# Six of eight gate/up K-tiles of an expert in three passes, low parts written over the raw weights, three slots per weight piece

## What is computed

```python
def rms_norm(x, g):
    y = xf * lax.rsqrt(jnp.mean(xf * xf, axis=-1, keepdims=True) + EPS)
    return y * g
def hier_moe(h, w_rg, b_rg, w_re, b_re, w_g, w_u, w_d):
    ...
    hid = jax.nn.silu(jnp.einsum('bsd,edf->bsef', h, w_g)) * jnp.einsum('bsd,edf->bsef', h, w_u)
    hid = hid * gate[..., None]
    return jnp.einsum('bsef,efd->bsd', hid, w_d)
for l in range(DEPTH):
    x = x + hybrid_mixer(rms_norm(x, norm_mix_g[l]), ...)
    x = x + hier_moe(rms_norm(x, norm_ffn_g[l]), ...)
```

## Time and profile before

| | |
|---|---|
| median of 3 runs | 1399.3 us (1398.26 to 1400.98) |
| profiled execution, its own time | 1398.75 us |
| its span | 1396.8 us |
| TensorE matmul busy | 1363.1 us (98%), granted clock 0.993 |
| VectorE / ScalarE / GpSimd busy | 863.2 (62%) / 585.8 (42%) / 728.4 us (52%) |
| DMA | 224.28 MB, mean 161 GB/s |

### The profile page before, as it was taken

How to read it: one execution, slowest core, us unless ns; L and a number is a source line. 1 busy time by engine, 2 the same in 40 slices (tenths; PEclk the granted TensorE clock), 3 DMA queues, 4 the chain that set the end, 5 groups by cost and what they waited for, 6 DMA issues and landing times.

```text
span 1396.8 us, 19901 instructions
## 1 busy us (share of the span) xinstructions
PE 1363.1 (98%) x6916; PEld 1036.2 (74%) x6916; DVE 863.2 (62%) x2057; ACT 585.8 (42%) x1334; POOL 728.4 (52%) x587
## 2 busy tenths in 40 slices
PE   7999999999999999999889999999999999999997
PEld 5788877777777876767477888777777778667674
DVE  4487866656684347776346787666567741576772
ACT  4323333343433135676443432433434421466761
POOL 4566645445345634566555576454444455255663
PEclk9999999999999999999889999999999999999999
DMA  5436422222212659999732242222222128599995
GB/s 154 130 100 172 121 83 73 73 74 97 90 61 76 232 217 318 340 360 350 190 118 76 61 135 81 75 76 74 89 80 90 61 88 292 213 330 350 346 348 130
DMA packets 148570, 224.28 MB, mean 161 GB/s; under 512 B 18635, under 2 KB 95877, under 8 KB 148463
## 3 DMA queue, kind: packets, MB, share of 16 engines
q1 hardware_dynamic: 136030, 197.59, 43.6%
q0 software_dynamic: 9936, 16.81, 5.1%
q10 hardware_dynamic: 2496, 8.52, 1.6%
HBM read 215.47 MB, written 31.25 MB: 177 GB/s over the span
## 4 chain that ended last, share of the span: by engine, by line
PE 92%; DVE 4%; ACT 1%; POOL 1%; DMA 1%; issue 1%; SPq 0%; POOLq 0%; ACTq 0%; DVEq 0%
PE bank L895 22%; PE bank L897 21%; PE bank L896 21%; PE bank L1200 9%; PE bank L1071 4%; PE bank L1083 3%; PE bank L1104 2%; PE bank L1152 2%; PE bank L1024 1%; PE bank L1094 1%; DVE probs L1913 1%; PE bank L1037 1%; POOL w_lo L769 1%; PE bank L1162 1%; PE bank L1360 0%
## 5 line engine op out<-in xcount | busy, mean ns | idle before, releaser
L769 POOL TENSOR_TENSOR w_lo<-raw,w_hi 128x512 fp32r<-128x512 f32 (+2 forms) x288 | 359.2, 1268 | 16.4 <-ACT w_hi L1641 4.6
L763 POOL TENSOR_SCALAR w_hi<-raw 128x1024 fp32r<-128x1024 f32 (+2 forms) x142 | 149.4, 1052 | 417.3 <-PE bank L897 414.5
L896 PE MATMUL bank<-w_hi,hT_lo 128*128 128x512 f32 (+2 forms) x696 | 258.8, 372 | 0.0
L895 PE MATMUL bank<-w_lo,hT_hi 128*128 128x512 f32 (+2 forms) x576 | 216.8, 376 | 2.1 <-DVE hT_lo L1738 1.2
L897 PE MATMUL bank<-w_hi,hT_hi 128*128 128x512 f32 (+2 forms) x576 | 211.8, 368 | 0.0
L895 PE MATMUL bank<-hT_lo,w_hi 128*128 128x512 f32 x384 | 159.5, 415 | 0.0
L897 PE MATMUL bank<-hT_hi,w_hi 128*128 128x512 f32 x384 | 150.7, 393 | 0.0
L896 PE MATMUL bank<-hT_hi,w_lo 128*128 128x512 f32 x384 | 150.2, 391 | 0.0
L896 PEld LDWEIGHTS bank<-w_hi,hT_lo 128*128 128x128 f32 x696 | 131.6, 189 | 20.3
L1200 PE MATMUL bank<-work,ptmp 128*128 128x512 f32 x288 | 129.4, 593 | 1.0 <-ACT ptmp L1565 1.0
L895 PEld LDWEIGHTS bank<-w_lo,hT_hi 128*128 128x128 f32 x576 | 108.7, 189 | 28.0 <-issue 8.7
(11 more groups left out here) (331 smaller groups left out, 2651.4 us busy)
## 6 DMA issues: line engine op xcount, KB each, us to landing
work<-in_w_ff_gate SPq DMA_DIRECT2D x66, 512.0 KB
work<-in_w_ff_up SPq DMA_DIRECT2D x66, 512.0 KB
work<-in_w_ff_down SPq DMA_DIRECT2D x33, 1024.0 KB
raw<-in_w_gate SPq DMA_DIRECT2D x48, 512.0 KB, 3.8
raw<-in_w_in SPq DMA_DIRECT2D x40, 512.0 KB, 3.6
raw<-in_w_branch SPq DMA_DIRECT2D x24, 512.0 KB, 3.6
raw<-in_w_out SPq DMA_DIRECT2D x16, 512.0 KB, 3.9
normed_dram<-mixed ACTq DMA_DIRECT2D x8, 512.0 KB, 2.7
```

Of the source, the lines that this page charges most:

```text
L763: nc.gpsimd.tensor_scalar(w_hi[:, two, :, 0:w], raw[:, slot, :, 0:w], 1.0, 0.0, ALU.mult, ALU.add).then_inc(split_hi, 1)
L769: last = nc.gpsimd.tensor_tensor(w_lo[:, two, kk, 0:w], raw[:, slot, kk, 0:w], w_hi[:, two, kk, 0:w].bitcast(F32), ALU.subtract)
L895: nc.tensor.matmul(out_ap, s_hi, m_lo, start=start, stop=False)
L896: nc.tensor.matmul(out_ap, s_lo, m_hi, start=False, stop=False)
```

## The change

Six of eight gate/up K-tiles of an expert go in three passes where four did (tiles 2 to 7, before 4 to 7), from expert 1 on instead of expert 2 (`SPLIT_FROM = 2`, `FIRST_SPLIT = 1`); tiles are split in pairs. Low parts are written over the raw weights they come from (`slots_low` are the same bytes as `slots_raw`), so a slot comes free only when TensorE has used it. There are nine slots, three per piece: the ring's six, two in `X` and one in `w_lo`. For the two in `X` the loads wait until `X` is stored, turned and scaled. Gate/up weights are loaded with two consecutive rows of 256 floats per partition, one run of 2 KB instead of 1 KB. The norm's gain, before a scale on ScalarE and VectorE in each expert, is now multiplied into `xn` once by GpSimd (8 products of 128x512, reading every second element so that the columns stand in the order of the weights' rows; one of them after the power step). The high parts of expert 1's tiles are made by ScalarE before `et_out(0)`, and their low parts by GpSimd before its loop over the experts. The one-hot tiles and token picks move to other places of `hT_lo`.

```diff
-RING = 6
+SLOTS_OF_PART = ((0, 3, 6), (1, 4, 7), (2, 5, 8))
+AHEAD = 3
+
+ROW_RUN = 2
 
 EXPERT_AT = [PER_GROUP * (e % N_GROUPS) + e // N_GROUPS for e in range(N_EXPERTS)]
 PIECES = 3
 
-FIRST_SPLIT = 2
-
-PIECE_ORDER = [(2, 0), (2, 1), (2, 2), (3, 0), (3, 1), (4, 1)]
-for before in range(2, N_EXPERTS - 1):
-    PIECE_ORDER += [(e, part) for e, part in ((before + 2, 0), (before + 1, 2), (before + 3, 1)) if e < N_EXPERTS]
-
-
-def split_count(e):
-
-    return 4 * (e - FIRST_SPLIT + 1)
+FIRST_SPLIT, SPLIT_FROM = 1, 2
+SPLIT_PAIRS = (8 - SPLIT_FROM) // 2
+
+PIECE_ORDER = [(2, 2), (2, 0), (2, 1), (3, 0), (3, 1)]
+for e in range(4, N_EXPERTS):
+    PIECE_ORDER += [(e, 0), (e, 1), (e - 1, 2)]
+PIECE_ORDER.append((N_EXPERTS - 1, 2))
...
+        X_low = low_twin("X_low", [P, TT, D_MODEL], F32R)
         X = sb("X", [P, TT, D_MODEL])
...
+        w_lo_raw = low_twin("w_lo_raw", [P, 2, UNIT_KT, 512], F32)
...
-        both = hT_hi[:, 4, 0:64].rearrange("p (t e) -> p t e", t=TT)
-        pick_token = hT_hi[:, 4, 64:192].rearrange("p (k t e) -> p k t e", k=2, t=TT)
+        both = hT_lo[:, 5, 0:64].rearrange("p (t e) -> p t e", t=TT)
+        pick_token = hT_lo[:, 5, 64:192].rearrange("p (k t e) -> p k t e", k=2, t=TT)
...
+        ffn_gain = probs[:, 0:2, :].rearrange("p a n -> p (a n)")
...
-        slot_onehot = hT_hi[:, 5:7, :].rearrange("p a (t s) -> p a t s", s=CAPACITY)
+        slot_onehot = hT_lo[:, 6:8, :].rearrange("p a (t s) -> p a t s", s=CAPACITY)
...
-        et_hi, et_lo = hT_hi[:, 0:2, :], hT_hi[:, 2:4, :]
-        gu_hi_bufs = [[oT_hi[:, k, :] for k in range(4)], [hT_lo[:, k, :] for k in range(4)]]
-        gu_lo_bufs = [[oT_lo[:, k, :] for k in range(4)], [hT_hi[:, 5, :], hT_hi[:, 6, :], hT_hi[:, 7, :], hT_lo[:, 6, :]]]
+        et_hi = hT_hi[:, 0:4, :].rearrange("p (b a) n -> p b (a n)", b=2)
+        et_lo = ptmp_low[:, :, :].rearrange("p (b a) n -> p b (a n)", b=2)
+        gu_hi_bufs = [[oT_hi[:, 0:2], oT_hi[:, 2:4], oT_lo[:, 0:2], oT_lo[:, 2:4]],
+                      [hT_lo[:, 0:2], hT_lo[:, 2:4], hT_hi[:, 4:6], hT_hi[:, 6:8]]]
+        slots_raw = [work[:, n].rearrange("p k n -> p (k n)") for n in range(6)]
+        slots_raw += [X[:, 0:2, :].rearrange("p a n -> p (a n)"), X[:, 2:4, :].rearrange("p a n -> p (a n)"),
+                      w_lo_raw[:, :, :, :].rearrange("p a k n -> p (a k n)")]
...
+            return src.rearrange("a (j p k) n -> p (a j) (k n)", p=P, k=ROW_RUN)
...
-                    slot, old = n % RING, e - 2
+                    old = e - AHEAD
                     if old >= 0 and part == 0:
                         sp.wait_ge(first_half, old + 1)
-                    elif old >= 0 and part == 1 and splits(old):
-                        sp.wait_ge(gu_lo, split_count(old))
                     elif old >= 0 and part == 1:
                         sp.wait_ge(gu_done, old + 1)
                     elif old >= 0:
-                        sp.wait_ge(down_lo, old + 2)
-                        if old:
-                            sp.wait_ge(down_lo_dve, old)
+                        sp.wait_ge(down_done, 2 * (old + 1))
                     if part < 2:
                         for half, w in enumerate((w_ff_gate, w_ff_up)):
                             src = layer_of(w, l)[:, EXPERT_AT[e], part * 512:(part + 1) * 512, :]
-                            sp.dma_start(gate_up_piece(slot)[:, half],
-                                         src.rearrange("a (k p) n -> p (a k) n", p=P)).then_inc(piece_in[slot], 16)
+                            sp.dma_start(gate_up_piece(e, part)[:, half].rearrange("p (j k) n -> p j (k n)", k=ROW_RUN),
+                                         in_runs(src)).then_inc(arrived(e, part), 16)
                     else:
-                        sp.dma_start(work[:, slot].rearrange("p (k c) n -> p k (c n)", k=2),
+                        sp.dma_start(down_rows(e),
...
                 sp.wait_ge(g_free, 4 * OUT_CHUNK)
+                sp.dma_start(ffn_gain, layer_of(norm_ffn_g, l).broadcast_to([P, D_MODEL])).then_inc(gain_in, 16)
...
+                    if (e, part) == (2, 0):
+                        sp.wait_ge(x_stored, 16 * TT)
+                        sp.wait_ge(x_gained, 2 * TT)
+                        sp.wait_ge(nt_done, 2 * KT)
                     load_piece(e, part)
...
-                        if i < 2:
+                        at = N_EXPERTS + i
+                        if i < AHEAD:
                             used, per = ((first_half, 1), (gu_done, 1), (down_done, 2))[part]
-                            sp.wait_ge(used, per * (N_EXPERTS - 1 + i))
+                            sp.wait_ge(used, per * (at - AHEAD + 1))
                         else:
                             used, per = ((e_gu, 1), (e_gu, 1), (e_down, 2))[part]
-                            sp.wait_ge(used, per * (i - 1))
...
+                def gain_step(t, c):
+                    pool.wait_ge(g_free, 4 * (OUT_CHUNK + c) + t + 1)
+                    cols = slice(c * 512, (c + 1) * 512)
+                    in_order = lambda rows: rows.rearrange("p (a n k) -> p a k n", n=P, k=ROW_RUN)
+                    nc.gpsimd.tensor_tensor(xn[:, t, cols].rearrange("p (a k n) -> p a k n", n=P, k=ROW_RUN),
+                                            in_order(X[:, t, cols]), in_order(ffn_gain[:, cols]),
+                                            ALU.mult).then_inc(x_gained, 1)
+
+                pool.wait_ge(gain_in, 32)
+                for t in range(TT):
+                    gain_step(t, 0)
+                for t in range(TT - 1):
+                    gain_step(t, 1)
                 pool.wait_ge(ms_done, TT + 1)
                 pow_step(row_rs[:, 1, :], row_ms[:, 1, :], TT).then_inc(rs_done, 1)
+                gain_step(TT - 1, 1)
...
-                            last = nc.gpsimd.tensor_tensor(w_lo[:, c, f, :], rows[:, f, c * 512:(c + 1) * 512],
+                            last = nc.gpsimd.tensor_tensor(down_low(e)[:, f, c * 512:(c + 1) * 512],
+                                                           rows[:, f, c * 512:(c + 1) * 512],
                                                            w_hi[:, c, f, :].bitcast(F32), ALU.subtract)
...
+                for n, (part, kk, kt) in enumerate(split_tiles()):
+                    pool.wait_ge(gu_hi, n + 1)
+                    for k in range(2):
+                        last = nc.gpsimd.tensor_tensor(
+                            gate_up_low(1, part)[:, :, kk + k, :], gate_up_piece(1, part)[:, :, kk + k, :],
+                            pair_hi_of(1, kt)[:, k, :].bitcast(F32).rearrange("p (h n) -> p h n", h=2), ALU.subtract)
+                    last.then_inc(gu_lo, 1)
...
+                if e and first_native(e):
+                    pe.wait_ge(et_act, copied(e))
...
+                for kt in range(KT):
+                    part, kk = divmod(kt, 4)
+                    if kk == 0:
+                        pe.wait_ge(arrived(e, part), loaded(e, part))
+                    rows = slice(kt * P, (kt + 1) * P)
+                    if kt < first_native(e):
+                        if e == 0 and kt < 4:
+                            pe.wait_ge(et_first, kt + 1)
                         if e == 0 and kt == 2:
                             turn_rest_of_first()
                         if e == 0 and kt == 4:
                             pe.wait_ge(et_dve, 1)
+                        last = nc.tensor.matmul(G[e % 2][:, :], et[:, e % 2, rows], gate_up_piece(e, part)[:, :, kk, :],
+                                                start=(kt == 0), stop=(kt == KT - 1))
+                    else:
+                        pair = (kt - SPLIT_FROM) // 2
+                        if kt == SPLIT_FROM:
+                            pe.wait_ge(et_dve, e + 1)
+                        if (kt - SPLIT_FROM) % 2 == 0:
+                            pe.wait_ge(gu_lo, split_pairs(e - 1) + pair + 1)
+                        last = three(G[e % 2][:, :], et_hi[:, e % 2, rows], et_lo[:, e % 2, rows],
+                                     pair_hi_of(e, kt)[:, (kt - SPLIT_FROM) % 2, :], gate_up_low(e, part)[:, :, kk, :],
+                                     kt == 0, kt == KT - 1)
+                    if kk == 3:
+                        last.then_inc(gu_done if part else first_half, 1)
...
+                native = P * min(4, first_native(e))
+                if native:
+                    nc.scalar.activation(et[:, e % 2, 0:native], S[0][:, 0:native], ACT.Copy).then_inc(et_act, 1)
                 if splits(e):
+                    if native < 512:
+                        nc.scalar.activation(et_hi[:, e % 2, native:512], S[0][:, native:512],
+                                             ACT.Copy).then_inc(et_hi_done, 1)
                     act.wait_ge(et_turned, 2 * e + 2)
-                    nc.scalar.activation(et_hi[:, e % 2, :], S[1][:, :], ACT.Copy).then_inc(et_hi_done, 1)
```

(75 more changed lines are left out.)

118 lines of the change are left out of this document (59 added, 59 removed).

## The result

The changed kernel takes **1414.15 us** (median of 4 runs, 1413.64 to 1414.25), the kernel before beside it 1399.62 (1398.26 to 1400.98). The ratio is 1.0104, 95% interval 1.0091 to 1.0117: 1% slower. The forecast was 1389, range 1386 to 1396. The profiled execution has a span of 1412.4 us, 15.6 more than before.

What follows compares the result with a forecast made beforehand. TensorE was taken as the bound, with DMA right behind. From the profiled 1398.75 us: less 11.0 for three-pass tiles, less 1.0 for ScalarE waits, plus 2.0 at stage starts, 1388.75; forecast 1389, range 1386 to 1396.

Steps and rivals of the forecast that it cites:

- The middle of the stage: Mid expert stage: TensorE sets the pace, other engines and DMA stay hidden; period per expert falls from 10.06 to 9.74 us.
- my bounds for the price of a tile: TensorE, gate/up: each tile changed to three passes saves 0.162 us; 0.005 us per matmul shifts the total 1.0 us either way.
- Rival (b): Mid-stage: DMA or VectorE becomes the bound, period stays at 10.06 us; 1398, no change that can be told; chance 0.09.
- the 358 in the prediction: DMA: HBM limit per core about 358 GB/s, so loads would need 9.94 us per expert, hidden by the head start.
- I take 1.0 us per layer: Start of the expert stage: added stall of 1.0 us per layer, 2.0 in all, bounds 0 and 7.
- The wait that I priced, for the third pair of low parts: TensorE in expert 1 waits for GpSimd's third pair: 0.9 us with a gather slip of 1.5, 3.4 with 4.
- Hidden: VectorE: its products and new low parts finish before they hold up TensorE, with about 2 us to spare mid-stage.
- The gathers slip by 0 to 4 us. I take 1.5: Stage start: expert 2's 3.1 MB of loads beside the xn stores delay the last store, and so the gathers.
- The strided products: GpSimd, before the power step: seven gain products at 1.27 to 1.5 us each; above 1.43, power is late by 7c - 10.0.
- Expert 1's saving of 1.0 us: TensorE, expert 1 gate/up: six tiles go from native to three passes, each saving 0.162 us.
- Rival (c): Stage start: strided products cost 2.54 us each, losing 6 to 8 us per layer; 1399 to 1403; chance 0.07.
- my own signs of being wrong: Products over 1.9 us, a period near 10, or transposes of experts 1 and 2 waiting for gathers landed late among loads.

Runs made afterwards that it cites:

- native_gathers_gain: Changed kernel with expert 1 native, expert 2's loads behind the first two gathers, and two gain products instead of one after the power step: 1388.01 us.
- before_plus_two_input: Kernel before plus six unused back-to-back GpSimd subtractions of two SBUF inputs, behind the low parts of expert 0's down weights: 1414.38 us.
- before_plus_one_input: Kernel before plus seven GpSimd multiplications by a constant, one SBUF input, behind the low parts of expert 0's down weights: 1413.52 us.
- lows_after_sum: Changed kernel with GpSimd waiting until tile_sum is made before it starts expert 1's low parts: 1402.14 us.

## Why the prediction was wrong

- **The middle of the stage: right.** No idle time, no wait of ScalarE for weights in the late experts, three slots and 369 GB/s enough. The period is 9.71 us where I had 9.74, since two tiles save 0.35 us and not 0.32: 5.0 us gained in each layer where 14 x 0.32 = 4.5 were forecast. That is at the good end of my bounds for the price of a tile. Rival (b) is out. The Trainium skill (DMA: Bandwidth & Descriptors, the section on the measured bandwidth) gives some 358 GB/s per core for two cores that stream at once, and up to 425 for one alone; this kernel runs on one core, and its 369 lies between them. So the 358 in the prediction was no limit here.
- **"I take 1.0 us per layer": the step that failed.** The start lost 13.3 us in layer 0, up to expert 1's first native matmul (542.78 against 529.51), beyond even the bound of 7 for both layers. The wait that I priced, for the third pair of low parts, doesn't occur in the trace; TensorE waits for `tile_sum` instead, a path that the prediction doesn't mention. I had summed GpSimd's and ScalarE's own times and asked only when each result is ready. Of VectorE I asked only about the products with `up` and its own low parts ("Hidden"); that the router's rest, ahead of `tile_sum`, runs beside GpSimd's six low parts I didn't look at. That is 6.9 of the 13.3 us. A sign of it lay in the profile: I quoted GpSimd's slower pair beside VectorE's low parts, and weighed it for GpSimd and for one L2184, not for small VectorE operations beside a long run of GpSimd. A plainer sign I didn't look up: L2077 took 0.94 us in the kernel before, and ended at 524.14 with GpSimd's four low parts (524.10).
- **"The gathers slip by 0 to 4 us. I take 1.5": mis-sized.** The slip was 6.2 us (522.79 against 516.57). The stores took 7.8 us to land, not 2.7, and were issued 1.6 later. I had put all bytes into one sum; but a store of 0.5 MB lands late among the loads, and the gathers behind it land late among them again. Nor did mid-stage need this head start of the loads of expert 2: with them held back until the gathers had landed, the period stays at 9.68 and 9.74 us (native_gathers_gain).
- **The strided products: price right, consequence missed.** 10.45 / 7 = 1.49 us, inside my 1.27 to 1.5, and so past the 1.43 at which the room is filled, which made 0.4 us by my own formula. It was 1.6, since the run also held off VectorE's sum of squares (2.10 against 0.69), for which the power step waits. That a step of 8 bytes is on the cheap side (the Trainium skill, GPSIMD Engine Reference, performance pitfalls) agrees: 1.49 us, 17% above 1.27, and not half as much again (the 1.27 is a subtraction, the 1.49 a multiplication, so the stride's own share is an estimate).
- **The clock: left out.** I priced waits at their length. Behind them 12 native records cost 1.7 us more, eight transposes 0.9 and four native records 1.0 in layer 0: 3.6 us, beside 10.7 of waits (6.1, 2.9 and 1.7 us).
- **Expert 1's saving of 1.0 us:** only 0.2 came (the last line of the table above), since its four native records ran 1.0 us longer at the lower clock. Its wait of 0.5 us for ScalarE is gone, inside the stretch before.
- **Rival (c), slower,** had the side right and the mechanism wrong: it rested on products of 2.54 us. Of my own signs of being wrong only one came near: a transpose did wait for gathered rows that landed late among the loads, but it was expert 0's.

## What to carry to other kernels

Work given to an idle GpSimd isn't free where VectorE has operations with two SBUF inputs. Here these stood until the next gap in GpSimd's run, those of 4 and 16 columns as well as the one of 512. So look for a small VectorE operation that feeds the engine that bounds the kernel, and put GpSimd's run behind it; gaps in the run gave back less than half (6.8 of some 15 us). Loads fetched ahead belong behind the small stores and gathers that the next stage waits for. Price a wait of TensorE together with the matmuls behind it, which may run at the lower clock.

## What the runs showed of the hardware

- A VectorE operation with two SBUF operands of 16 columns took 7.96, 8.25 and 8.03 us beside a back-to-back GpSimd run of two operands or of one (after, before_plus_two_input, before_plus_one_input), and 1.1 to 2.2 us when the run had gaps; 0.17 us outside such runs.
- A VectorE copy and an operation with a constant, 8 columns, took 1.20 and 1.33 us beside GpSimd's low parts (lows_after_sum), 0.17 us outside them. Reductions took 0.17 us beside the run with gaps.
- Stores of 0.5 MB landed in 7.8 us beside loads and in 2.7 us with the loads held back.
- A GpSimd product that reads every second float took 1.49 us, a contiguous subtraction of the same size 1.27.
- A core alone moved 369 GB/s over 40 us of the stage.
